# A hybrid decoder layer on one core: recurrence gates in 64x64 quarters of the array, and five joints between stages rewritten

## The reference

```python
h = rmsnorm(x, norm1_g)
xa, ga, q, k, v, gate_a, gate_b = split(h @ w_in)            # 8704 columns
xc = causal_dwconv(xa, ...)                                  # width 4
r = sigmoid(einsum('btnd,nde->btne', xc_blocks, wa) + ba)    # 16 blocks of 64 x 64
i = sigmoid(einsum('btnd,nde->btne', xc_blocks, wx) + bx)
a = exp(-8 * r * softplus(-lam)); u = sqrt(1 - a*a) * i * xc
h_t = a_t * h_(t-1) + u_t                                    # scan over time
branch_a = (h_t * gelu(ga)) @ w_br_a
branch_b = dilated_attention(q, k, v, caches) @ w_br_b
x = x + (sigmoid(gate_a) * branch_a + sigmoid(gate_b) * branch_b) @ w_out
up = causal_dwconv(rmsnorm(x, norm2_g) @ w_up, ...)          # width 3, 6144 columns
y = x + (gelu(gf) * vf) @ w_down
```

## Time and profile before

| | us |
|---|---|
| median of 3 runs (1208.29 to 1215.1) | 1209.48 |
| profiled execution, its own time | 1207.88 |
| its span, first to last instruction | 1206.1 |
| TensorE busy | 1190.7 |
| VectorE busy | 659.5 |
| ScalarE busy | 457.8 |
| GpSimd busy | 160.3 |

### The profile page before, as it was taken

The page is one execution under the profiler, slowest core; times in us unless marked ns, Lnnn a source line. Parts: engine busy times, 40 slices in busy tenths (PEclk is TensorE's granted clock), DMA queues, the critical chain, the costliest instruction groups (busy, mean ns, idle before and its releaser), DMA issues.

```text
span 1206.1 us, 21188 instructions
## 1 busy us (share of the span) xinstructions
PE 1190.7 (99%) x8793; PEld 1159.3 (96%) x8793; DVE 659.5 (55%) x1330; ACT 457.8 (38%) x709; POOL 160.3 (13%) x250
## 2 busy tenths in 40 slices
PE   9999999999999999999999999999999999999998
PEld 7989999999999999999999999999999999999998
DVE  6554443543532346575645457888428884378831
ACT  6434444434433356757533344222212222122221
POOL 2265134143131000000010020000100001000010
PEclk9999999999999999999999999999999999999999
DMA  8565245245232222222162222333232222222231
GB/s 242 139 183 161 78 121 163 76 121 148 76 94 71 59 82 70 72 87 62 46 198 76 75 82 71 88 86 87 75 87 84 74 86 83 79 87 83 74 102 52
DMA packets 182948, 117.14 MB, mean 97 GB/s; under 512 B 6932, under 2 KB 175528, under 8 KB 182856
## 3 DMA queue, kind: packets, MB, share of 16 engines
q1 hardware_dynamic: 172320, 89.70, 26.5%
q0 software_dynamic: 10544, 26.43, 7.9%
q10 hardware_dynamic: 10, 0.01, 0.0%
HBM read 107.66 MB, written 8.45 MB: 96 GB/s over the span
## 4 chain that ended last, share of the span: by engine, by line
PE 94%; DMA 2%; DVE 2%; POOL 1%; ACT 1%; issue 0%; ACTq 0%; DVEq 0%
PE ps L628 64%; PE ps L607 18%; PE ps L760 2%; PE ps L837 1%; DMA kc<-in_cache_k_g 1%; PE ps L724 1%; PE ps L698 1%; PE ps L738 1%; PE ps L685 1%; DMA w_raw<-in_w_br_a 1%; PE ps L765 1%; PE ps L899 0%; PE ps L710 0%; PE ps L650 0%; POOL kc L476 0%
## 5 line engine op out<-in xcount | busy, mean ns | idle before, releaser
L628 PE MATMUL ps<-h,w_s 128*128 128x288 f32 x3840 | 518.6, 297 | 0.0
L628 PEld LDWEIGHTS ps<-h,w_s 128*128 128x128 f32 x3840 | 513.3, 189 | 1.2 <-issue 0.2
L1324 DVE TENSOR_TENSOR w_s<-w_raw,w_s 128x1024 fp32r<-128x1024 f32 (+1 forms) x161 | 195.7, 1216 | 198.8 <-ACT w_s L955 198.0
L955 ACT ACTIVATE w_s<-w_raw 128x1024 fp32r<-128x1024 f32 (+1 forms) x161 | 167.4, 1040 | 351.0 <-PE ps L628 347.4
L607 PE MATMUL ps<-w_s,h 128*128 128x384 f32 x1152 | 217.5, 341 | 1.3 <-DVE h L1354 0.8
L607 PEld LDWEIGHTS ps<-w_s,h 128*128 128x128 f32 x1152 | 198.8, 188 | 3.4 <-issue 1.7
L628 PE MATMUL ps<-g_hi,w_s 128*128 128x288 f32 x768 | 136.3, 297 | 1.6 <-DVE g_lo L1758 1.6
L628 PEld LDWEIGHTS ps<-g_hi,w_s 128*128 128x128 f32 x768 | 113.5, 189 | 1.9 <-ACT g_hi L1288 1.8
L628 PE MATMUL ps<-g_lo,w_s 128*128 128x288 f32 x384 | 82.2, 296 | 0.0
L628 PEld LDWEIGHTS ps<-g_lo,w_s 128*128 128x128 f32 x384 | 61.9, 189 | 0.0
L569 POOL DMA_DIRECT2D out<-f_row x12 | 6.2, 518 | 414.4 <-ACT f_row L1295 414.4
(11 more groups left out here) (285 smaller groups left out, 1413.4 us busy)
## 6 DMA issues: line engine op xcount, KB each, us to landing
w_raw<-in_w_in SPq DMA_DIRECT2D x65, 512.0 KB, 4.0
w_raw<-in_w_up SPq DMA_DIRECT2D x48, 512.0 KB, 3.9
w_raw<-in_w_down SPq DMA_DIRECT2D x24, 512.0 KB, 3.8
kc<-in_cache_k_g POOLq DMA_DIRECT2D x48, 128.0 KB, 3.0
vc<-in_cache_v_g POOLq DMA_DIRECT2D x12, 512.0 KB, 6.1
w_raw<-in_w_br_a SPq DMA_DIRECT2D x8, 512.0 KB, 4.0
w_raw<-in_w_out SPq DMA_DIRECT2D x8, 512.0 KB, 3.9
x_tok<-in_x_prompt SPq DMA_DIRECT2D x4, 512.0 KB, 7.4
```

Source lines behind the costliest of these rows:

```text
L628: last = mm(pu[u % 2][:, 512 * a:512 * a + HALF], w[:, part, k, :], x[:, k, HALF * a:HALF * (a + 1)], start=(k == 0 and i == 0), stop=(k = ...
L955: A(w_s[:, ring(u), 0, 0:nkt[u], :], w_raw[:, u % NRAW, 0:nkt[u], :], ACT.Copy).then_inc(hi_ready, 1)
L1324: TT(w_s[:, ring(u), 1, 0:nkt[u], :], w_raw[:, u % NRAW, 0:nkt[u], :], w_s[:, ring(u), 0, 0:nkt[u], :], ALU.subtract).then_inc(lo_ready, 1)
```

## The change

- **Gates.** `wa` and `wx` hold only the 64x64 blocks, 64 columns a group; the two memsets of zeros on GpSimd are gone. `gate_products` issues eight matmuls of 64 rows by 64 columns instead of four of 128x128. For each half `a` the four are: block j of `wa` from input rows 64j to output rows 64j, and block j of `wx` from input rows 64j to the other half of the output rows. ScalarE takes the input gate back with two Tanh instructions of 64 partitions each, that cross the halves. The bias `bx` is loaded with its 64-blocks swapped, by two transfers.
- **Head.** `x_hi(1)` and `x_lo(1)` go ahead of `x_stat(2)` and `x_scale(2)`. The transposes of class 2 move from slice 2 to slice 4 of row tile 1.
- **First unit of `w_br_a`.** It is loaded, split and waited for in two halves, and `branch_b(6)` goes ahead of its `lo_split`.
- **Second norm.** For the last slice, the square goes ahead of `h_hi` on ScalarE, and the low part of the sum of squares goes ahead of a `lo_split` on VectorE.
- **Last round.** Slices 0 to 6 of unit 0 are followed by slices 0 to 2 of unit 1, and then come slice 7 of unit 0, slices 3 and 4 of unit 1, `state_rows` and slices 5 to 7. The `y_rows` of an output tile go in behind slice 0 or slice 4 of a later unit. The last unit does its 288-column halves one after the other, and half of its output tile is added, transposed and stored while the second half is computed.

```diff
@@ before line 35
+LB = 64
@@ before line 78
-    return u + 1 + 3
+    return u + 1 + 3 + (u >= U_BA)
@@ before line 110
-X_AT = {0: 4, 1: 2, 2: 2, 3: 2}
+X_AT = {0: 4, 1: 4, 2: 2, 3: 2}
@@ before line 242
-        wa = at(o_r + VEC, "wa", [P, KT, P])
-        wx = at(o_r + VEC + 4 * KB, "wx", [P, KT, P])
+        wa = at(o_r + VEC, "wa", [P, KT, LB])
+        wx = at(o_r + VEC + 2 * KB, "wx", [P, KT, LB])
@@ before line 301
+        raw_late, half_done, x2_half = sem("raw_late"), sem("half_done"), sem("x2_half")
@@ before line 418
+                if u == U_BA:
+                    for k, s in ((slice(0, 4), raw_in[u % NRAW]), (slice(4, KT), raw_late)):
+                        sp.dma_start(w_raw[:, u % NRAW, k, :], units[u][:, k, :]).then_inc(s, 16)
+                    return
@@ before line 439
-            for m in range(KT):
+            def store_y(m, n0, n1):
+                sp.dma_start(out[0][0].rearrange("(n p) d -> p n d", p=P)[:, n0:n1, m * P:(m + 1) * P],
+                             y_tok[:, n0:n1, m * P:(m + 1) * P]).then_inc(y_out, 16)
+                if n1 == 4:
+                    sp.dma_start(out[1].rearrange("b t d -> (b t) d")[:, m * P:(m + 1) * P],
+                                 y_tok[0:NS, 4, m * P:(m + 1) * P]).then_inc(y_out, 16)
+            for m in range(KT - 1):
-                sp.dma_start(out[0][0].rearrange("(n p) d -> p n d", p=P)[:, :, m * P:(m + 1) * P],
-                             y_tok[:, 0:4, m * P:(m + 1) * P]).then_inc(y_out, 16)
-                sp.dma_start(out[1].rearrange("b t d -> (b t) d")[:, m * P:(m + 1) * P],
-                             y_tok[0:NS, 4, m * P:(m + 1) * P]).then_inc(y_out, 16)
-            sp.wait_ge(y_out, 32 * KT)
+                store_y(m, 0, 4)
+            for q in range(2):
+                sp.wait_ge(yt_rdy, KT + q)
+                store_y(KT - 1, 2 * q, 2 * q + 2)
+            sp.wait_ge(y_out, 32 * KT + 16)
-                               (slice(V_BA, V_BX), "lru_ba"), (slice(V_BX, V_LAM), "lru_bx"),
+                               (slice(V_BA, V_BX), "lru_ba"),
+            blocks = lambda ap, j: ap.rearrange("p (c j e) -> p c j e", j=2, e=LB)[:, :, j, :]
+            for j in range(2):
+                pool.dma_start(blocks(nat_v[V_BX:V_LAM, :], j), blocks(t["lru_bx"], 1 - j)).then_inc(s_nat, 16)
@@ before line 522
-            pool.memset(wa[:, :, :], 0.0).then_inc(gw_zero, 1)
-            pool.memset(wx[:, :, :], 0.0).then_inc(gw_zero, 1)
-            pool.wait_ge(gw_zero, 2)
-                    pool.dma_start(buf[64 * j:64 * j + 64, :, 64 * j:64 * j + 64], src[j]).then_inc(gw_in, 16)
+                    pool.dma_start(buf[LB * j:LB * (j + 1), :, :], src[j]).then_inc(gw_in, 16)
@@ before line 651
-                pe.wait_ge(s_nat, 16 * 9)
+                pe.wait_ge(s_nat, 16 * 10)
@@ before line 832
-                for i, w in enumerate((wa, wx)):
-                    for a in range(2):
-                        last = mm(ps[2 + i][:, 512 * a:512 * a + LW // 2], w[:, c, :],
-                                  xc[:, c % 2, a * LW // 2:(a + 1) * LW // 2], start=True, stop=True)
+                for a in range(2):
+                    for i, w in enumerate((wa, wx)):
+                        for j in range(2):
+                            rows, o = slice(LB * j, LB * (j + 1)), LB * (j ^ i)
+                            last = mm(ps[2 + i][o:o + LB, 512 * a:512 * a + LW // 2], w[rows, c, :],
+                                      xc[rows, c % 2, a * LW // 2:(a + 1) * LW // 2], start=True, stop=True)
@@ before line 850
-            unit(U_BA, y_hi, y_lo)
+            looped_unit(U_BA, KT, parts(U_BA) - 1, freed(U_BA), y_hi, y_lo, None,
+                        {4: lambda: pe.wait_ge(lo_ready, parts(U_BA))})
@@ before line 900
-            def y_rows(m):
+            def y_rows(m, n0=0):
-                for n in range(4):
+                for n in range(n0, 4):
+            def first_rows(m):
+                pe.wait_ge(x2_half, 1)
+                for n in range(2):
+                    last = tr(ps[2][:, n * P:(n + 1) * P], x2[:, m, n * P:(n + 1) * P], ident)
+                last.then_inc(yt_ps, 1)
+            def down_products(u, k, halves_, start, stop):
+                r = NRND - 1
+                for i, (part, x) in enumerate(((0, g_hi[r % 2]), (0, g_lo[r % 2]), (1, g_hi[r % 2]))):
+                    for a in halves_:
+                        last = mm(pu[u % 2][:, 512 * a:512 * a + HALF], w_s[:, ring(u), part, k, :],
+                                  x[:, k, HALF * a:HALF * (a + 1)], start=(start and i == 0), stop=(stop and i == 2))
+                return last
+            def last_round_begin():
+                u, v, k1 = down_unit(NRND - 1, 0), down_unit(NRND - 1, 1), PPR - 1
+                pe.wait_ge(lo_ready, parts(u))
+                pe.wait_ge(acc_free[u % 2], freed(u))
+                for k in range(k1):
+                    pe.wait_ge(g_hi_rdy, NPAIR - k1 + k)
+                    pe.wait_ge(g_lo_rdy, NPAIR - k1 + k)
+                    down_products(u, k, range(2), k == 0, False)
+                pe.wait_ge(lo_ready, parts(v))
+                pe.wait_ge(acc_free[v % 2], freed(v))
+                for k in range(PPR):
+                    if k == 3:
+                        pe.wait_ge(g_hi_rdy, NPAIR)
+                        pe.wait_ge(g_lo_rdy, NPAIR)
+                        down_products(u, k1, range(2), False, True).then_inc(unit_done, 1)
+                    if k == 5:
+                        state_rows(NRND - 1)
+                    last = down_products(v, k, range(2), k == 0, k == k1)
+                last.then_inc(unit_done, 1)
+            def last_unit():
+                u = down_unit(NRND - 1, KT - 1)
+                pe.wait_ge(lo_ready, parts(u))
+                pe.wait_ge(acc_free[u % 2], freed(u))
+                for a in range(2):
+                    for k in range(PPR):
+                        if k == 5:
+                            y_rows(KT - 2) if a == 0 else first_rows(KT - 1)
+                        last = down_products(u, k, (a,), k == 0, k == PPR - 1)
+                    last.then_inc(unit_done if a else half_done, 1)
@@ before line 926
-                down(r, 0)
-                state_rows(r)
+                    down(r, 0)
+                    state_rows(r)
-                    for m in range(1, KT):
-                        down(r, m)
-                        y_rows(m - 1)
-            y_rows(KT - 1)
+                    last_round_begin()
+                    for m in range(2, KT - 1):
+                        unit(down_unit(r, m), g_hi[r % 2], g_lo[r % 2], None,
+                             {1: lambda: y_rows(0) if m == 2 else None, 5: lambda: y_rows(m - 1)})
+                    last_unit()
+            y_rows(KT - 1, 2)
@@ before line 952
+                if u == U_BA:
+                    A(w_s[:, ring(u), 0, 0:4, :], w_raw[:, u % NRAW, 0:4, :], ACT.Copy).then_inc(hi_ready, 1)
+                    act.wait_ge(raw_late, 16)
+                    A(w_s[:, ring(u), 0, 4:KT, :], w_raw[:, u % NRAW, 4:KT, :], ACT.Copy).then_inc(hi_ready, 1)
+                    return
@@ before line 1098
+            x_hi(1)
-            x_hi(1)
@@ before line 1195
-                gate = lambda i, dst: A(dst[:, :].rearrange("p (h n) -> p h n", h=2),
-                                        ps[2 + i][:, :].rearrange("p (h n) -> p h n", h=2)[:, :, 0:LW // 2], ACT.Tanh,
-                                        scale=0.5, bias=sp4[:, 2 + i, c:c + 1])
-                gate(0, g_r).then_inc(l_gr, 1)
-                gate(1, g_i).then_inc(gate_read, 1)
+                def gate(i, dst, to, frm):
+                    return A(halves(dst[to, :]), halves(ps[2 + i][frm, :])[:, :, 0:LW // 2], ACT.Tanh,
+                             scale=0.5, bias=sp4[frm, 2 + i, c:c + 1])
+                gate(0, g_r, slice(0, P), slice(0, P)).then_inc(l_gr, 1)
+                gate(1, g_i, slice(0, LB), slice(LB, P))
+                gate(1, g_i, slice(LB, P), slice(0, LB)).then_inc(gate_read, 1)
@@ before line 1265
-                A(h_hi[:, c, :], x2[:, c, :], ACT.Identity, scale=vt[:, c, V_N2:V_N2 + 1]).then_inc(xg2_hi, 1)
+                if c < KT - 1:
+                    A(h_hi[:, c, :], x2[:, c, :], ACT.Identity, scale=vt[:, c, V_N2:V_N2 + 1]).then_inc(xg2_hi, 1)
+                if c == KT - 1:
+                    A(h_hi[:, c, :], x2[:, c, :], ACT.Identity, scale=vt[:, c, V_N2:V_N2 + 1]).then_inc(xg2_hi, 1)
@@ before line 1293
+            def y_take_first(m):
+                act.wait_ge(yt_ps, m + 1)
+                A(y_tok[:, 0:2, m * P:(m + 1) * P], ps[2][:, 0:2 * P].rearrange("p (n d) -> p n d", n=2), ACT.Copy).then_inc(yt_rdy, 1)
+            def y_take_rest(m):
+                act.wait_ge(yt_ps, m + 2)
+                A(y_tok[:, 2:4, m * P:(m + 1) * P], ps[3][:, 2 * P:SEQ].rearrange("p (n d) -> p n d", n=2), ACT.Copy)
```

(30 more changed lines are left out.)

## The result

The changed kernel has a median of 1196.76 us over 4 runs (1195.86 to 1197.83), against 1208.88 us over 4 runs of the kernel before. The ratio is 0.9889 with a 95% interval of 0.9855 to 0.9924, that is 9.2 to 17.5 us faster; in per cent 1.1. The profiled execution took 1197.17 us, 10.7 less than the 1207.88 of before.

What follows compares the result with a forecast made beforehand. TensorE was taken as the bound; 5.4 (gates) + 0.45 + 1.16 + 0.59 + 1.80 + 0.55 = 9.95 us off the profiled 1207.88 gave 1197.9, and the median was forecast at 1199. The range was 1195.5 to 1205 us.

Steps and rivals of the forecast that it cites:

- from the execution to the median: Whole kernel: profiled execution 1197.9 us, old one 1.6 us below its median, so median 1199.5, said as 1199.
- Bound: Whole kernel: TensorE, busy 1190.7 of 1206.1 us at full clock; the wait for cached keys stays at 4.9 us.
- Gates: Recurrence stage: four quarters work at once, 1.34 us a group instead of 2.02, saving 5.4 us in all.
- Rivals 2: Recurrence stage's gates: quarters don't overlap, 4.37 us a group, 18.8 us lost, 1223 us in all; chance 0.05.
- 4 (1.67 us a group): Recurrence stage's gates: overlap holds but switching costs twice what the strips show, 1201.6 us in all; chance 0.05.
- Rival 1: Gates: quarters work only in pairs, two blocks sharing a bank; 2.35 us a group, 2.6 lost, 1207 us; chance 0.10.
- Third Tanh: ScalarE in the recurrence stage: 0.65 us more a group, 5.2 in all, cover about zero before `hi_split`, costed at nothing.
- Head: First row tiles: x_lo(1) no longer stands behind x_scale(2); gain 0.45 us, bounds 0 and 0.95; tile 2 late next.
- First unit of w_br_a: Wait before this unit: with halved transfer and branch_b(6) done at about 615.8, all 1.16 us go.
- Second norm: Wait before the square sums: with the square moved ahead of h_hi, gain 0.59 us, bounds 0.3 and 0.7.
- Last round and end: Last units and output: 1.80 us of wait go; end nets 0.55, 1.35 earlier less 0.77 for transposes; together 2.35.
- rival 3: Stage joints: TensorE waits again in last round or recurrence stage, half of 4.55 us lost, 1201.3; chance 0.08.

Runs made afterwards that it cites:

- e9: Kernel before with 512 KB of masks moved ahead of class 2's transfer; row tile 0 to row tile 2 took 13.27 us against 11.96, span 1207.7.
- e10: Changed kernel with the same 512 KB of masks moved ahead of class 2; row tile 0 to row tile 2 took 11.48 us against 11.50, span 1194.3.
- e1: Kernel before with only the quartered gates added; median 1204.99 us over 10 executions, ratio 0.9961.
- e12: Changed kernel with class 2's transposes at slice 2, keys 2 and 3 transposed earlier, VectorE's copies moved ahead; 1197.64 us over 6 executions, ratio to before 0.9906.
- e2: Changed kernel with the gates of before; median 1201.95 us over 9 executions, ratio to before 0.9943.
- e5: Changed kernel with two more unused Tanh ahead of each group's gates; the 24 recurrence units took 165.13 us against 164.37, whole 1197.61 us, one execution.
- e6: Changed kernel with the first unit of w_br_a loaded and split whole, branch_b(6) still ahead; U_BB to w_br_a took 27.08 us against 25.59.
- e7: Changed kernel with the first unit of w_br_a in halves but branch_b(6) behind both splits; U_BB to w_br_a took 26.57 us against 25.59.

## What held of the prediction, and the step that failed

**The step that failed: from the execution to the median.** The median came at 1196.76 us for 1199. The terms of the sum held in the traces: 10.15 us for 9.95. The profiled execution came at 1197.17 for 1197.9, and 0.64 us of that gap lies in the start of the span and in the stretch with attention, which the change doesn't touch. What failed is the sentence "a median made alike would be 1199.5". It takes the joints' prices of one execution for all, and carries the 1.6 us between the old kernel's profiled execution and its median over to the new kernel. The runs showed otherwise. The changed kernel's profiled execution was 0.4 us above its median, not 1.6 below. Between the executions the medians gained 12.1 us, 2.0 more than the five parts in the traces. In the medians the joints alone gave 6.9 us (5.0 to 8.7), above the 4.55 of the sum, while the gates alone gave 4.7 (2.9 to 6.5), which holds the 5.4.

The mis-sized terms are the two whose price follows a landing. The head was put at 0.45 and measured 0.46, but 1.79 with class 2 late on both sides (e9, e10); `w_br_a` was put at 1.16, and its old code lost another 0.27 in e1 and 0.55 in e9. The rest stays open, and the clock has a share in it. Of the 36 executions of the kernel before that ran beside e1, e9 and e12 (one of 4149 us left out), the 10 with a mean granted clock of 1.000 have a median of 1207.28 us, and the 17 at 0.998 or below one of 1210.31. The four of the changed kernel are at 0.999 or 1.000. But e1 had 3 of 10 executions at 0.998 or below, and e2 2 of 9, so neither half of the change by itself is shown to keep the clock up.

**Bound.** Right. TensorE stayed the bound at the full clock, and the 10.15 us came from its own work and from the named waits. The wait for cached keys was forecast to stay at 4.9 and was 4.0; over the traces it varies by itself.

**Gates.** Right in mechanism and nearly in size: 5.23 of 5.4 us. One reading was wrong without harm. The working says that no 64-row tile is in the trace of before. There are some, the eight transposes of the samples at 30.27, but they use the same rows one after the other and say nothing of overlap. The step of 0.2525 held, as did the reading of the column strips: 0.16 us in the chain's gate piece and 0.19 behind it, where the forecast took 0.16 and 0.17. Records of four quarters start together:

```profile
435.83 0.69 PE L644 MATMUL ps<-h,w_s 128*128 128x288 f32 x4
436.45 0.47 PE L856 MATMUL ps<-xc,wa 64*64 64x300 f32 x2
436.47 0.47 PE L856 MATMUL ps<-xc,wx 64*64 64x300 f32 x2
436.76 0.42 PE L856 MATMUL ps<-xc,wa 64*64 64x300 f32 x2
...
437.28 0.42 PE L856 MATMUL ps<-xc,wx 64*64 64x300 f32 x2
437.63 0.53 PE L644 MATMUL ps<-h,w_s 128*128 128x288 f32 x2
```

Each line is a pair of records (x2), one per block of the gate. The first four start within 0.02 us.

Rivals 2 (no overlap) and 4 (1.67 us a group) fall with the measured 1.37 us a group, 2.02 less 5.23/8. Rival 1 had quarters in pairs only, because the two blocks of `wa` lie in different rows and write one bank of PSUM. They ran at once. The Trainium skill ("TensorEngine Tiling (Array Packing)", Gotcha 1) says that different row tiles can't access the same bank simultaneously; with the two blocks in different output partitions of that bank, this trace doesn't agree, and the measurement decides. What happens when two row tiles write the same partitions of a bank wasn't run.

**Third Tanh.** Hidden, as forecast, but for the wrong amount. Its two instructions of 64 partitions:

```profile
582.14 0.76 ACT L1273 ACTIVATE g_r<-ps,sp 128x600 f32<-128x600 f32 x1
582.92 1.53 ACT L1273 ACTIVATE g_i<-ps,sp 64x600 f32<-64x600 f32 x2
```

From the start of the first gate's Tanh to the end of the last it is 2.31 us in every group, against 1.41 before: 0.90 more, not 0.65. I had used the distance between two starts. The third instruction takes 0.77, and the first two no longer overlap: 0.78 from start to start instead of 0.65. And the cover that the working put at about zero was not what counts: it stopped at the `hi_split` and its own idle time, while the low part had 3.1 us. The working also put VectorE's delay at nothing because "the scan feeds only the next group". It cost nothing, but that is the place where the cover is thin: from `xc` to the next gates it fell from 1.08 to 0.82 us, and e5 used it up.

**Head.** The 0.45 us came as 0.46, with the wait moved to row tile 2 at 0.38 instead of 0.3. Row tile 1 started 5.91 us after row tile 0 instead of 6.85, 0.94 of 0.95. The term is mis-sized all the same, not for this trace but for the median. I took the landing of class 2 as it was in one execution: ScalarE waited 0.57 us for it there. With landings 1.4 us later on the old side and 2.4 on the new, the same edit is worth 1.79 us (e9, e10), and where a late landing comes with a drop of the clock as in e1, the old order loses 3.8 us against its own lucky execution. The forecast for the median should have had a term for the operation that has its input and stands behind one that waits for a transfer.

**First unit of w_br_a.** All 1.16 us went. My working named the accumulator and the landing both, and e6 and e7 show both: with either cure taken out TensorE waits again, 1.6 or 0.8 us. In the changed kernel `branch_b(6)` started at 609.73, 3.0 us before the unit at 612.73, and ended 2.2 us before it. The forecast had it done 3.2 us before; it took the end of the product for the end of the addition.

**Second norm.** 0.65 us for 0.59. The `sq_lo` ended 0.5 us before the square sums began:

```profile
724.51 0.76 DVE L1802 TENSOR_TENSOR sq_lo<-sq_sum,sq_hi 128x576 fp32r<-128x576 f32 x1
...
725.80 0.42 PE L903 MATMUL ps<-sq_hi,ones_r 128*128 128x288 f32 x2
```

**Last round and end.** 2.65 us for 2.35. The end, from the start of the last addition:

```profile
1190.96 0.46 DVE L1872 TENSOR_TENSOR x<-ps,x 128x288 f32<-128x288 f32 x1 [2.96 <-PE ps L943]
1192.06 0.38 ACT L1383 ACTIVATE y_tok<-ps 128x256 f32<-128x256 f32 x1 [1.91 <-PE ps L931]
1192.34 0.26 ACT L1384 ACTIVATE y_tok<-ps 64x128 f32<-64x128 f32 x1
```

Addition to second copy's start is 1.38 us against 2.71 in the earlier trace rows, so 1.33 earlier, forecast 1.35. From that copy's end to the end of the span it was 2.97 us and is now 2.67. This 0.31 (by unrounded times) the forecast left out. The last large transfer carries two row tiles instead of four, which may be the reason; no run tested it. The remainder, 2.65 - 1.64 = 1.01, is the last round's 1.80, whose wait for `g_lo` is gone, less 0.79 for the transposes that now stand ahead of the last product, forecast 0.77. No addition came late (rival 3 falls).

## What to carry to other kernels

Here a small block-diagonal product was worth moving into as many quarters of the array as it had blocks. Price such a move by the records of one quarter, and a fixed cost per visit read from any rows that already tile the array. Where an operation with its input ready stands behind one that waits for a transfer, the order costs more than the profiled execution shows, because the landing moves from execution to execution. Look at the landings of several executions before carrying a sum of waits over to a median, and before comparing two kernels at a joint. And where a wait names one releaser, look for what else is late by nearly as much before pricing its cure: at the `w_br_a` joint neither cure alone removed the wait.

## What the runs showed of the hardware that I had not expected

- Two 64-row tiles wrote one PSUM bank at once in different partitions, with steps of 0.2525 us, as if alone.
- Using the array in quarters cost about 0.35 us a visit (0.16 and 0.19), for 16 records and for 32, and for two quarters and for four.
- A Tanh of 64 partitions by 600 took 0.76 us, as one of 128 partitions (0.76), also when it writes the other half of the partitions. Three in a row on 128, 64 and 64 partitions start 0.78 us apart, two on 128 partitions 0.65.
- TensorE's clock fell in e1 after a pause of 2.9 us in the head (granted clock 0.53 from 22.5 to 26 us), and the 3.5 us at that level held 16 records instead of 25. After the pause of 2.1 us in e9 it stayed at 1.0. In e2 it fell after a pause of 2.7 us (0.50 from 90.8 to 94.2 us), and the changed kernel, with a longest pause of 2.5 us for keys, kept 1.0 there.
- One and the same transfer of 512 KB of weights, issued at the same point of the program, took 9.15, 9.43, 9.71 and 10.01 us in four executions.
